# Seven block products for eight in the MLP's input projections of an fp32 two-block kernel

## What is computed

```python
u, v, z = jnp.split(h @ w_in, 3, axis=-1)      # h: 1024 x 1024, w_in: 1024 x 6144
u = jax.nn.gelu(u)
v = layer_norm(jax.nn.gelu(v), ln_g, ln_b)      # over the 2048 columns of V
v = v.reshape(bsz, n_chunks, CHUNK, A_GROUPS, A_GROUP_CH)
s = jnp.einsum('gts,bnsgc->bntgc', w_causal, v) + b_s.T[:, :, None].astype(v.dtype)
y = u * s.reshape(bsz, s_len, A_WIDTH) * jax.nn.silu(z)
return y @ w_out                                # w_out: 2048 x 1024
```

## Time and profile before

| | us |
|---|---|
| median of 3 runs | 2620.71 (2619.92 to 2620.92) |
| span of the profiled execution | 2617.6 |
| PE busy | 2575.0 |
| DVE busy | 1258.0 |
| POOL busy | 1053.0 |
| ACT busy | 856.4 |

### The profile page before, as it was taken

How to read it: one execution, slowest core, us unless ns; L and a number is a source line. 1 busy time by engine, 2 the same in 40 slices (tenths; PEclk the granted TensorE clock), 3 DMA queues, 4 the chain that set the end, 5 groups by cost and what they waited for, 6 DMA issues and landing times.

```text
span 2617.6 us, 41022 instructions
## 1 busy us (share of the span) xinstructions
PE 2575.0 (98%) x16272; PEld 2081.5 (80%) x16272; DVE 1258.0 (48%) x2357; ACT 856.4 (33%) x1687; POOL 1053.0 (40%) x1310
## 2 busy tenths in 40 slices
PE   7999999999999999999999999999999999999999
PEld 6777787877777777777788888888887888777787
DVE  4225343344857567576524533533445006577743
ACT  4434353536323333332013301211113114455531
POOL 3232323323433232321467333544444556454452
PEclk9999999999999999999999999999999999999999
DMA  4111111111201011112332211111111114210122
GB/s 148 37 48 38 52 42 49 41 45 41 65 26 57 26 46 38 33 55 96 137 125 89 73 41 49 41 49 49 41 47 43 49 49 137 65 33 25 33 107 87
DMA packets 210126, 153.80 MB, mean 59 GB/s; under 512 B 5264, under 2 KB 192016, under 8 KB 209424
## 3 DMA queue, kind: packets, MB, share of 16 engines
q1 hardware_dynamic: 186256, 106.44, 13.8%
q10 hardware_dynamic: 23680, 44.74, 4.7%
HBM read 128.10 MB, written 23.07 MB: 58 GB/s over the span
## 4 chain that ended last, share of the span: by engine, by line
PE 90%; DVE 6%; ACT 2%; POOL 1%; issue 1%; DMA 0%; ACTq 0%; SPq 0%; DVEq 0%; POOLq 0%
PE gemm L633 23%; PE gemm L635 22%; PE gemm L634 22%; PE scores L688 2%; PE weighted L715 1%; PE scores L1230 1%; PE weighted L1254 1%; PE probs_t L700 1%; PE scores L1124 1%; PE probs_t L946 1%; PE probs_t L1240 1%; PE scores L850 1%; PE max_rows L939 1%; PE scores L950 1%; ACT inv_x L2291 1%
## 5 line engine op out<-in xcount | busy, mean ns | idle before, releaser
L584 POOL CAST w_hi<-w_raw 128x512 fp32r<-128x512 f32 x346 | 246.6, 713 | 1445.7 <-PE gemm L635 1379.4
L633 PE MATMUL gemm<-h_hi,w_hi 128*128 128x512 f32 x1904 | 778.1, 409 | 0.9 <-DVE h_lo L1734 0.9
L635 PE MATMUL gemm<-h_hi,w_lo 128*128 128x512 f32 x1904 | 744.5, 391 | 0.0
L634 PE MATMUL gemm<-h_lo,w_hi 128*128 128x512 f32 x1904 | 742.9, 390 | 0.0
L586 POOL TENSOR_TENSOR w_lo<-w_raw,w_hi 128x256 fp32r<-128x256 f32 x692 | 595.6, 861 | 54.7
L633 PEld LDWEIGHTS gemm<-h_hi,w_hi 128*128 128x128 f32 x1904 | 358.3, 188 | 80.5 <-issue 14.2
L635 PEld LDWEIGHTS gemm<-h_hi,w_lo 128*128 128x128 f32 x1904 | 357.3, 188 | 77.2
L634 PEld LDWEIGHTS gemm<-h_lo,w_hi 128*128 128x128 f32 x1904 | 358.7, 188 | 64.0 <-issue 1.9
L1720 DVE TENSOR_TENSOR scaled_product<-gemm,norm_rstd 128x512 f32<-128x512 f32 x108 | 74.7, 692 | 301.3 <-PE gemm L635 298.8
L1382 DVE CUSTOM_DVE_ANT_0 neg_logits<-scores,bias_tile 128x128 f32<-128x128 f32 (+1 forms) x192 | 67.6, 352 | 148.6 <-PE scores L688 142.7
L633 PE MATMUL gemm<-xn_hi,w_hi 128*128 128x512 f32 x288 | 117.7, 409 | 1.9 <-DVE xn_lo L1876 1.7
(11 more groups left out here) (536 smaller groups left out, 4333.7 us busy)
## 6 DMA issues: line engine op xcount, KB each, us to landing
w_raw<-in_w_in SPq DMA_DIRECT2D x73, 512.0 KB, 3.9
w_raw<-in_a_w_in SPq DMA_DIRECT2D x48, 512.0 KB, 3.7
gates_scratch<-o_f ACTq DMA_DIRECT2D x32, 256.0 KB, 2.0
merge_gates<-gates_scratch ACTq DMA_DIRECT2D x4, 2048.0 KB, 10.2
w_raw<-in_a_w_out SPq DMA_DIRECT2D x16, 512.0 KB, 3.6
w_raw<-in_b_w_in SPq DMA_DIRECT2D x16, 512.0 KB, 3.9
x_rows<-in_x SPq DMA_DIRECT2D x8, 512.0 KB, 8.4
w_raw<-in_w_out SPq DMA_DIRECT2D x8, 512.0 KB, 3.7
```

What stands on the lines that cost most here:

```text
L584: Q(pool.tensor_copy(weight_part(u, 0, ks), raw[:, s, ks, :]))
L633: pe.matmul(dst, w_high, hi(k, h), start=first, stop=False)
L634: pe.matmul(dst, w_high, lo(k, h), start=False, stop=False)
L635: m = pe.matmul(dst, w_low, hi(k, h), start=False, stop=last)
```

## The change

Two neighbouring units (256 columns) become one product of 2 x 2 blocks: K in two halves of 512, tokens in two halves of 512, columns in two of 128. Strassen's scheme (in Winograd's form) makes it of seven block products, each of 4 k tiles x 3 matmuls. Eight units of V stay as they were (`V_PLAIN`); the other eight and all of U and Z, 40 units, are 20 pairs (`SEVENS`, four of them V; the other 16 are one unit of U with one of Z). Products 2, 3 and 6 are accumulated in PSUM onto the product two before them in the same bank.

Around this:

- The block sums of h (T) are made in place of x by DVE, split by ACT and DVE (`t_sums`, `t_highs`, `t_lows`) during V's plain groups. The block sums of the weights are made for each pair by DVE (three) and POOL (one). ACT makes the high parts of the weights, which POOL's cast made before.
- An eviction is now a sum of products with what was kept (`first_product`, `first_two`), and the root a second step (`rooted`).
- There is no room for V: its rows go to DRAM in pieces (`piece_out`), the statistics are taken from 128-column pieces, and each tile comes back for its pair (`v_again`) and is normalised on ACT (`v_normed`). y is stored to DRAM and read back for the output product (`y_again`). The y tile, gate and u times s of a pair are made in the next pair.

```diff
+            def seven_product(m, o):                       # PE
+                b, key = bank_of(seven(m), o), (seven(m), o)
+                pe.wait_ge(E("seven_low"), 7 * m + o + 1)
+                pe.wait_ge(g_evac[b], out_no[key])
+                for k in range(4):
+                    high, low = seven_moving(o, k)
+                    pe.matmul(G[b][:], w_high[:, k, :], high, start=k == 0 and o not in (2, 3, 6), ...)
+                    pe.matmul(G[b][:], w_high[:, k, :], low, ...)
+                    t = pe.matmul(G[b][:], w_low[:, k, :], high, ...)
...
             for i in range(16):                            # PE, U and Z
-                for h in range(2):
-                    gemm_half(U_UZ + 2 * i + 1, h, *H2)
+                m = V_SEVENS + i
+                seven_product(m, 0)
...
+                for o in range(2, 6):
+                    seven_product(m, o)
+                pe.wait_ge(E("v_tile"), i + 1)
                 for n in range(8):
+                    t = pe.matmul(S2[:, n * P:n * P + P], vt[i % 2][:, n, :], wsT[:, i // 2, :], start=True, stop=True)
+                seven_product(m, 6)
...
+            def v_normed(i):                               # ACT
+                act.wait_ge(bias_in[i % 2], BIAS_LOADS + 16 * (i // 2 + 1))
+                for n in range(8):
+                    tile = vt[i % 2][:, n, :]
+                    A(a.activation(tile, tile, ACT.Identity, bias=stat[:, 344 + n:345 + n], scale=stat[:, 336 + n:337 + n]), E("v_tile") if n == 7 else None)
...
+                if i:                                      # ACT, in pair i
+                    act.wait_ge(E("y_mlp"), i)
+                    act.dma_start(y_d[i - 1], yr[:]).then_inc(E("up_in_y_out"), 16)
+                else:
+                    load_table(ACT.Sqrt)
+                    act.wait_ge(E("y_var"), PAIRS + 1)
+                    A(a.activation(stat[:, 336:344], stat[:, 336:344], ACT.Sqrt), E("y_sd"))
+                    load_table(ACT.Gelu_apprx_tanh)
+                    act.wait_ge(E("y_rstd"), PAIRS + 1)
+                v_normed(i)
...
             def v_stats(g):                                # DVE
-                if g in (1, 3) or g % 4 == 3:
+                for n in (2 * g, 2 * g + 1):
+                    piece_stats(n)
+            def piece_stats(n):
+                for c in range(4):
+                    V(v.bn_stats(v_stat[:, 4 * h + c, i, :], v_piece[n % 4][:, c, :]))
...
+                    if k < 8:                              # SP, reading y back
+                        wait_seven(sp, SEVENS - 1, (1, 3, 4, 5)[k // 2])
+                    else:
+                        sp.wait_ge(E("y_mlp"), 16)
```

More of the change, by code:

```diff
@@ L355, in build @@
         slot_before, last_in = {}, [None, None]
-        for u in range(U_END):
+        for u in (*range(U_S), *range(U_AO, U_END)):
             if u not in w_extra:
@@ L1092, in _ @@
             v_rows_of(2)
-            for g in range(4, 16):
+            for g in range(4, V_PLAIN):
                 for b, (i, h) in enumerate(V_GROUPS[g]):
@@ L1108, in _ @@
-            gemm_half(U_UZ, 0, *H2)
-            v_rows_of(15)
-            pe.wait_ge(E("rowsum"), 1)
-            for i in range(16):
-                for h in range(2):
-                    if (i, h) not in ((0, 0), (1, 0)):
-                        gemm_half(U_UZ + 2 * i, h, *H2)
-                for h in range(2):
-                    gemm_half(U_UZ + 2 * i + 1, h, *H2)
-                if i == 0:
-                    gemm_half(U_UZ + 2, 0, *H2)
-                pe.wait_ge(E("v_normed"), 5)
-                pe.wait_ge(E("v_normed_act"), 3)
+                        t = pe.matmul((PV, MB)[h][:], ones, wsT[:, 4 * h:4 * h + 4, :], start=True, stop=True)
@@ L1787, in _, with two_sum, three_sum @@
+            def two_sum(m):
+                dve.wait_ge(*emptied(seven(m), 0))
+                evict(m, 1, first_two[:], first_product[:], ALU.add)
+            def three_sum(m):
+                evict(m, 3, first_product[:], first_product[:], ALU.add)
             for k in range(KT):
@@ L1864, in _ @@
+            gate_z(15)
+            low_of_y(2)
+            times_u(15)
+            low_of_y(3)
+            y_tile(15)
+            for k in range(4, 16):
+                low_of_y(k)
             g_ = gain["a_post_g_2"]
@@ new lines, in _ @@
+            weight_high(0, 0)
+            v_gelu(V_PLAIN - 1, 0)
+            weight_high(0, 1)
+            v_gelu(V_PLAIN - 1, 1)
+            v_store(V_PLAIN - 2)
+            for o in range(2, 6):
+                weight_high(0, o)
+            for m in range(V_SEVENS):
+                if m:
+                    v_turned(m - 1, 3)
+                first_copy(m)
+                weight_high(m, 6)
+                weight_high(m + 1, 0)
+                if m:
+                    later_out(m - 1, 1)
+                    later_out(m - 1, 2)
+                else:
+                    v_store(V_PLAIN - 1)
+                v_turned(m, 0)
+                weight_high(m + 1, 1)
+                weight_high(m + 1, 2)
+                if m:
+                    later_out(m - 1, 3)
+                weight_high(m + 1, 3)
+                weight_high(m + 1, 4)
+                v_turned(m, 1)
+                later_out(m, 0)
+                weight_high(m + 1, 5)
+                v_turned(m, 2)
@@ L2454, in square @@
+            high_of_mlp(2)
+            turned(SEVENS - 1, 3, ug[:, hi_half], ug[:, hi_half], ACT.Gelu_apprx_tanh)
+            for k in range(3, 8):
+                high_of_mlp(k)
+            act.wait_ge(E("y_mlp"), 16)
+            act.dma_start(y_d[15], yr[:]).then_inc(E("up_in_y_out"), 16)
+            for k in range(8, 16):
+                high_of_mlp(k)
+            load_table(ACT.Sqrt)
             def square(src, k):
```

619 lines of the change are left out of this document (456 added, 163 removed).

## The result

| | before | after |
|---|---|---|
| median of the runs, us | 2620.82 (2619.92 to 2624.2, 4 runs) | 2636.51 (2632.27 to 2638.84, 4 runs) |
| ratio | | 1.0058, 95% interval 1.0043 to 1.0072 |
| span of the profiled execution | 2617.6 | 2630.2 |
| granted clock, mean of each run | 0.996 to 0.998 (runs of this kernel beside the experiments) | 0.990 to 0.994 |

Slower by 0.6%, where 2634 us and "slower" were forecast (range 2606 to 2654). The profiled execution of after is the fastest of its four (2632.27), so its 12.6 us over before are a little less than the medians' 15.7.

The account below looks back on a forecast made before the run. PE was taken as the bound, by matmul count times spacing. Terms: -54.4 + 34.0 + 6.8 + 12.7 + 2.6 + 3.0 + 8.7 = +13.4 us, so a span of 2631.0 and a median of 2634 us, range 2606 to 2654.

Parts of the forecast that it names:

- Step 1: U/Z pairs: V's tile is normalised too late, PE stops 2.27 us before the small products in 15 pairs, +34.0 us.
- Step 2: First U/Z pair: aggregations, root, table load and normalisations take 15.0 us against 8.16 covered, +6.8 us.
- Step 3: V's plain groups: DVE's added work makes a 14.6 us loop against PE's 11.80, so transposes wait for Gelu, +12.7 us.
- Steps 4 to 6: Three smaller losses: +2.6 us at h's low parts, +3.0 in V by sevens, +8.7 at the hand-over to the output product.
- The low parts of h: Ahead of V's plain groups: statistics of rows 0 delay the last two low parts of h, +2.6 us.
- V by sevens: V's four seven-product pairs: DVE's piece rows make it late for product 3's eviction, +3.0 us.
- The hand-over: Start of the output product: late low parts of y and its reading back from DRAM, +8.7 us.
- the third rival: POOL becomes the limit if DVE's 9 us count in full: 25.2 us a pair, 2666 us; chance 0.08 (POOL or more).
- Waits mostly covered: Rival: the U/Z chain is mostly hidden and the kernel gets faster, 2607 us, or 2570 to 2590 if wholly; chance 0.23.
- POOL becomes the bound: Rival: POOL's subtractions, slowed by DVE, take 25.2 us a U/Z pair, giving 2666 us; chance 0.08 (POOL or more).
- Products not back to back: Rival: two semaphore waits before each of 140 products cost 0.1 us each, +14 us; given little chance, no number.

Follow-up runs that it names:

- the shortened ones: Changed kernel without row statistics in V's plain groups 0 and 3 to 6, aggregating statistics of four units instead of sixteen; 2618.41 us, one run.
- the experiment above: Changed kernel with low parts 1 to 7 of y made ahead of the last pair's S, gate, u and y steps; 2633.88 us, ratio 1.0053.
- the edits together: Changed kernel with small products behind product 6, normalisation ahead of the y wait, statistics later in V's plain groups 4 to 7 and group 0; 2591.27 us.

## Why the prediction was right, and which of its steps were not

The sum was right to 0.8 us in the span of the profiled execution (2631.0 against 2630.2), which is the fastest of its four; the median was 2636.5 where 2634 was forecast (2633.8 over nine runs). Single terms were off by up to 6 us with both signs, so part of that is compensation, and luck. The kind of the loss was right: all the gain is there, and is given back in stops of PE behind other engines' program order.

**Step 1, the chain of a U/Z pair.** Place, releaser and count are right, the size 1.89 us a pair instead of 2.27, some 28 us instead of 34.0. Confirmed: DVE's five steps from 0.28 us after product 2, and 0.49 us for a normalisation with two pointers (eight take 4.18, predicted 4.17). Wrong: the y tile was put at 1.65, "and POOL starts its next subtraction at that moment". It took 1.23. POOL did start, at 1768.18, but that is 0.18 us behind DVE, and the slowing fell on POOL (two subtractions in 2.46 us, 1.55 alone), so 1.23 was the end of the range to take. And the link itself: the prediction had ACT stand for y; the high parts of the weights, in no term of it, hold ACT as long, so taking y out gave 0.37 a pair and not the wait. Had y been faster still, nothing would have been gained; "wrong above all if ACT receives the y tile earlier than 5.6 us after product 2" was too simple: it came 0.5 earlier, after 5.14, and ACT was not free for another 0.14. A stop also costs more than its wait, 0.30 us where 0.1 was put: the last matmul ahead runs for its whole 0.39 us where the next would follow after 0.23, and the small products then take 2.05 instead of 1.95.

**Step 2, the first pair.** 6.8 was too small: the wait is 8.15. Eight aggregations were taken from the earlier trace rows at 2.35, but these read 24 numbers a row and the changed kernel's 96, 4.95 us; the shortened ones took 2.35 and the wait fell by 2.19. The term was 2.6 too small, the wait only 1.35 above the forecast, since PE came to it 0.8 later itself (a wait of 0.45 for product 3's bank and its restart, in no term) and the steps ahead of the aggregations took 5.9 instead of 6.2. The table load, counted with 1.5, costs what it was put at (1652.99 to 1654.49). Behind the stop the small products took 3.66 instead of 1.95 us at half clock.

**Step 3, V's plain groups.** A loop of 14.8 was measured (1493.01 to 1507.78) against 14.6; the waits of 2.91 and 2.80 are the predicted 2.8 and 2.7. The third was 0.28 instead of 2.7: behind the stop of 2.80 the clock had fallen and PE came 1.6 later itself (13.6 us of work instead of 12.0), and that loop took only 13.9, since POOL stood idle and two of the T sums took 0.75 and 0.69 instead of 1.11. The fourth was 4.17 (4.0); the 0.5 for the first copy does not appear. In all 10.2 of waiting, and some 1.5 for each of the two falls of the clock behind it, where 12.7 was put: the sum is near, made up of other parts. That 2.5 us of the loop are DVE's waiting for ACT stood in the sum, but not that work could be put there.

**Steps 4 to 6.** The low parts of h: waits of 3.25 against 0.89, 2.4 (predicted 2.6). V by sevens: 1.5 of waits (3.0). The hand-over: 7.4 (8.7); the reading back, put at 2, had some 6 us to spare for its last tile, which landed 28 us after the last product. The prediction had 35.5, and its own numbers (4 MB from 13.5 us on, at 10.0 for 2 MB) give 33.5. The second K half was also not due as late as the experiment above supposed: PE came to it at 2037.8, not at 2050.

**The rest of the sum.** 1.6 us stand behind the output product, where 0 was put: 0.5 is a longer wait at the same place as before, and the clock was low there in this execution but not in the second profile of the same kernel (wait 1.7, clock 1.00; its last stretch is 436.1 us, as before).

**The rivals.** *Waits mostly covered* did not happen in this order of instructions, but its condition, a chain under 8.16 us, was right about what decides: with 2.72 more of cover, or the chain's ACT part moved into ACT's idle time, the time was 2604 and 2609, near the 2607 for another reason; the edits together, at 2591, are near the 2590 that it gave for a chain that vanished wholly. *POOL becomes the bound*: PE never waited for a low part of a weight; POOL was busy 14.6 of 22.7 us a pair (64%), and 71% at the shorter period. Here the prediction's own term was too large as well: it had POOL's 16 subtractions at 19.5 us a pair, and they took about 15.2 (eight rows of two, of 1.54 to 2.46), against 12.4 alone. DVE's 9 us cost POOL 2.8 and not 6.7, since much of them, the weight sums above all, fell into stretches where POOL waited for ACT's high parts and stood idle. The Trainium skill ("SBUF — State Buffer", section "SBUF: two separate sides") has the two engines take one port pair by an exclusive lock, so that the loser waits for the whole of the other. The trace nearly agrees where their steps met (last section), and the rival still did not come true: the prediction's "by that rule the third rival below would come true" counted all of DVE's steps as met. *Products not back to back*: in the timeline matmuls follow at 0.23 us over the boundary of two products.

## What to carry to other kernels

On an engine that bounds the time, an algorithm with fewer instructions is worth what it saves only if the work around it keeps its place: list for each resource that the bound engine takes (bank, tile) the chain through the other engines' program orders, and compare it with the work that now covers it, which has shrunk too. When a chain is too long, look for the instruction ahead of it that waits for something else, and move the step into the idle time in front; here four moves in the code were worth 43 us, and the work was the same. Take the price of an operation from a row of the same width of input, above all for reductions.

## What the runs showed of the hardware

**Stops of PE cost clock afterwards.** Before, the granted clock is 1.00 in all of U and Z. After, it falls behind the longer stops. By stretches of 4 us:

```profile
1544.00:1548.00 4.00, 2.71 (x12) 2.36 (x13) 0.49 (x1) 2.38 (x4) 0.97 (x2) 0.76 0.34 131
1548.00:1552.00 4.00, 4.00 (x16) 3.22 (x15) 1.10 (x2) 2.63 (x5) 3.61 (x6) 0.81 0.01 2
...
1656.00:1660.00 4.00, 1.25 (x6) 1.25 (x7) 0.38 (x1) 3.32 (x8) 0.05 (x1) 0.50 0.10 20
1660.00:1664.00 4.00, 4.00 (x20) 3.70 (x20) 0.00 (x0) 1.73 (x3) 2.88 (x4) 0.73 0.70 241
```

0.50 is the 1.2 GHz level. PE stood 4.17 us up to 1545.29 and 8.15 up to 1658.75. Behind the first the matmuls are 0.43 us apart instead of 0.23 for some 3 us; behind the second the small products take 3.66 us instead of 1.95:

```profile
1547.18 0.63 PE L1209 MATMUL gemm<-t_hi,w_lo 128*128 128x512 f32 x1
1547.61 0.63 PE L1207 MATMUL gemm<-t_hi,w_hi 128*128 128x512 f32 x1
```

The stops of 1.59 us that return every 22.7 us left it at 1.00, and so did the one of 2.91 at 1503. No term of the prediction had this. From the rows (1.6 and 1.5 us behind the two stops in V, 1.7 at the first pair's small products, some 1 behind the output product; at the hand-over PE waits again a moment later, so that slow matmuls there cost little) I estimate 6 us in the profiled execution. The runs of one kernel differ with it: the nine runs of after have mean clocks of 0.990 to 0.994, where before has 0.996 to 0.998. With the four edits together it was 0.994 to 0.996, in four runs within 4.9 us. Taking out the 14 stops in U and Z alone did not bring it back (0.990 to 0.993 with the small products behind product 6, 0.988 to 0.993 with the normalisation ahead of the high parts; spreads of 7.1 and 10.2 us). Moving the statistics in V's plain groups alone did in part (0.993 to 0.995, 11 runs within 3.3 us). That points at the stops of 2.8 to 4.2 us in V as the source of the spread. What decides in one execution whether the clock falls stays open: over all profiles it fell behind stops of 1.87 to 2.93 us in some places and not behind ones of 2.17, 2.57 and 2.91 in others, and never behind those of 1.59.

**Which engine pays when DVE and POOL meet: the one that starts second.** The u step (L2092) and the y step (L2096) have the same size and 1.23 us alone. The timelines of DVE and of POOL in one pair:

```profile
1762.40 1.68 DVE L2092 TENSOR_TENSOR mlp_y<-mlp_y,mlp_u 128x1024 f32<-128x1024 f32 x1
```

```profile
1762.28 2.41 POOL L688 TENSOR_TENSOR w_lo<-w_raw,w_hi 128x256 fp32r<-128x256 f32 x2
1768.18 2.46 POOL L688 TENSOR_TENSOR w_lo<-w_raw,w_hi 128x256 fp32r<-128x256 f32 x2 [3.50 <-ACT w_hi L2763]
```

DVE's u step starts 0.12 us behind a subtraction of POOL (0.74 alone, so 0.62 are left of it) and is 0.45 longer; the y step (1768.00) starts 0.18 ahead of one, keeps its 1.23, and POOL's two are 0.91 longer (1.05 were left). In the first case POOL's second subtraction waits for DVE in turn, hence its 2.41. With the small products behind product 6 the u step starts 0.46 behind POOL (0.28 left) and takes 1.36, 0.13 longer. In the three cases the second is held up by what was left of the first, less about 0.15 us. This pattern stands in nearly every pair of those profiles; no experiment moved one engine's start alone.
